# Two transformer blocks on one core: gates as one plus tanh, and the second group of Fox keys and queries split piece by piece

## What is computed

```python
h = rmsnorm(x, norm_mix)
q_a, k_a, v_a, f_a, q_b, kv_b, g_b, gate_a, gate_b = jnp.split(h @ w_in, ...)
log_f = log_sigmoid(f_a + b_forget)
o_a = fox_attention(q_a, k_a, v_a, log_f)      # 8 heads of 64, causal, decay by log_f
y_a = from_heads(o_a) @ w_o_fox
g = sigmoid(g_b)                               # weights of three NSA branches
o_n = nsa_attention(...)                       # compressed, selected, windowed
y_b = from_heads(o_n) @ w_o_nsa
mixed = sigmoid(gate_a) * y_a + sigmoid(gate_b) * y_b
x = x + mixed @ w_out
h = rmsnorm(x, norm_mlp)
x = x + square(relu(h @ w_up)) @ w_down
```

## Time and profile before

| | us |
|---|---|
| median of 3 runs | 2934.06 |
| lowest and highest | 2933.1, 2936.9 |
| the profiled execution | 2932.05 |
| its span, first to last instruction | 2930.2 |
| TensorE busy | 2775.1 |
| VectorE busy | 1503.6 |
| ScalarE busy | 1216.8 |
| mean granted clock of TensorE | 0.977 |

### The profile page before, as it was taken

One profiled execution on the slowest core, in us unless ns is written; L12 is line 12 of the kernel. 1 busy time (PEld: TensorE's weight loads), 2 busy tenths in 40 slices (PEclk: granted clock), 3 DMA queues, 4 the chain that ended last, 5 costly groups with the idle time before them and its releaser, 6 DMA issues.

```text
span 2930.2 us, 34957 instructions
## 1 busy us (share of the span) xinstructions
PE 2775.1 (95%) x13625; PEld 2282.6 (78%) x13625; DVE 1503.6 (51%) x2695; ACT 1216.8 (42%) x2169; POOL 132.2 (5%) x221
## 2 busy tenths in 40 slices
PE   7999999998999999989889999999989899999997
PEld 6777888886778888767777888888767677888886
DVE  6755433457554334566755643342566655553343
ACT  4553222245532222455656443242455756342231
POOL 1000000000000000011121000000010111000000
PEclk9899999999999999989999999999999999999999
DMA  4102232221022323211311223333212211333332
GB/s 128 41 23 87 97 96 99 95 82 45 23 90 95 100 94 101 83 50 58 94 44 44 87 88 99 95 100 94 83 41 75 80 37 51 93 101 94 100 94 79
DMA packets 186359, 231.42 MB, mean 79 GB/s; under 512 B 11874, under 2 KB 140356, under 8 KB 186196
## 3 DMA queue, kind: packets, MB, share of 16 engines
q1 hardware_dynamic: 184500, 225.95, 24.7%
q0 software_dynamic: 976, 1.32, 0.3%
q10 hardware_dynamic: 720, 1.92, 0.2%
HBM read 227.05 MB, written 2.11 MB: 78 GB/s over the span
## 4 chain that ended last, share of the span: by engine, by line
PE 79%; DVE 11%; ACT 5%; issue 4%; DMA 0%; POOL 0%; DVEq 0%; ACTq 0%; SPq 0%
PE bank L643 23%; PE bank L645 23%; PE bank L644 23%; DVE Wl L2110 2%; PE bank L803 1%; PE bank L858 1%; ACT Wh L1412 1%; DVE STT L2389 1%; PE bank L879 1%; PE bank L740 1%; DVE KAl L2814 1%; PE bank L880 1%; PE bank L921 1%; PE bank L1103 1%; PE bank L788 1%
## 5 line engine op out<-in xcount | busy, mean ns | idle before, releaser
L2110 DVE TENSOR_TENSOR Wl<-RAW,Wh 128x1024 fp32r<-128x1024 f32 (+3 forms) x434 | 511.3, 1200 | 388.8 <-ACT Wh L1412 388.0
L1412 ACT ACTIVATE Wh<-RAW 128x1024 fp32r<-128x1024 f32 (+3 forms) x434 | 438.6, 1033 | 367.7 <-PE bank L645 367.2
L643 PE MATMUL bank<-Hh,Wh 128*128 128x512 f32 (+1 forms) x976 | 396.3, 406 | 9.1 <-DVE Wl L2110 7.5
L645 PE MATMUL bank<-Hh,Wl 128*128 128x512 f32 (+1 forms) x976 | 385.9, 395 | 0.0
L644 PE MATMUL bank<-Hl,Wh 128*128 128x512 f32 (+1 forms) x976 | 385.5, 395 | 0.0
L643 PE MATMUL bank<-Wh,A 128*128 128x512 f32 x864 | 337.2, 390 | 0.0
L645 PE MATMUL bank<-Wh,A 128*128 128x512 f32 x864 | 336.3, 389 | 0.0
L644 PE MATMUL bank<-Wl,A 128*128 128x512 f32 x864 | 336.2, 389 | 0.0
L643 PE MATMUL bank<-HA,Wh 128*128 128x512 f32 x704 | 276.7, 393 | 7.0 <-DVE HA L2159 7.0
L645 PE MATMUL bank<-HA,Wl 128*128 128x512 f32 x704 | 275.6, 391 | 0.0
L644 PE MATMUL bank<-HA,Wh 128*128 128x512 f32 x704 | 275.5, 391 | 0.0
(11 more groups left out here) (371 smaller groups left out, 4357.3 us busy)
## 6 DMA issues: line engine op xcount, KB each, us to landing
RAW<-in_w_up_dram SPq DMA_DIRECT2D x108, 512.0 KB, 3.6
RAW<-in_w_down_dram SPq DMA_DIRECT2D x108, 512.0 KB, 3.8
RAW<-in_w_in_dram SPq DMA_DIRECT2D x90, 512.0 KB, 3.5
RAW<-in_w_gate_dram SPq DMA_DIRECT2D x44, 512.0 KB, 3.5
RAW<-in_w_out_dram SPq DMA_DIRECT2D x28, 512.0 KB, 3.8
RAW<-in_cmp_w_dram SPq DMA_DIRECT2D x16, 512.0 KB, 3.9
RAW<-in_w_o_fox_dram SPq DMA_DIRECT2D x8, 512.0 KB, 3.4
RAW<-in_w_o_nsa_dram SPq DMA_DIRECT2D x8, 512.0 KB, 3.4
```

Of the source, the lines that this page charges most:

```text
L643: pe.matmul(o, sh, mh, start=first, stop=False)
L645: return pe.matmul(o, sl, mh, start=False, stop=last)
L1412: sc.activation(M.Wh[:, v % NHL, 0:n], M.RAW[:, v % NRAW, 0:n], ACT.Copy).then_inc(G.w_hi, 1)
L2110: ve.tensor_tensor(M.Wl[:, v % NRAW, 0:n], M.RAW[:, v % NRAW, 0:n], M.Wh[:, v % NHL, 0:n].bitcast(F32), ALU.subtract).then_inc(G.w_lo, 1)
```

## The change

Two edits. The first: the sigmoids of the two gates become `tanh(x / 2)` on ScalarE, VectorE's product with the bank becomes `(tanh + 1) * bank` in one instruction, and the missing factor of one half is put into the split of the sum (MXh with a scale, MXl with a factor). The sigmoid of the branch weights at the forget gate stays. The second: for heads 4 to 7 the evacuation of a Fox key or query keeps only the product into TQ. Its pieces become a side of their own (`split_k`, `split_q`), begun there, which idles for one tick and then does one piece on each engine per tick. In TensorE's program idle sides of the same length keep the ticks in step. For heads 0 to 3 the pieces stay in one run, but each KAl piece now waits for its own KAh piece, where before two waited for the second of a pair.

```diff
-    def lin_t_units(name, kt, xh, xl, before=None, count=1):
+    def lin_t_units(name, kt, xh, xl, before=None, count=1, after=None):
...
+                    if after:
+                        after()
...
+        splits = []
+        lin_t(f"fk{l} 1", KD, M.Hh, M.Hl, after=lambda: splits.append(begin(idle(5))))
+        lin_t(f"fq{l} 1", KD, M.Hh, M.Hl, after=lambda: splits.append(begin(idle(3))))
         kc = lin_t_units(f"kc{l}", KD, M.Hh, M.Hl)
         next(kc)
+        drain(*splits)
...
-        def fox_q(c):
+        splits = []
+
+        def split_q(c, j, name):
+            yield
+            sc.wait_ge(*K.drained(name))
+            for x in range(2):
+                sc.activation(M.QA[c][0:64, 2 * j + x, :], M.TQ[64 * x:64 * x + 64, j, :], ACT.Copy).then_inc(*hi.up())
+                yield
+
+        def split_k(c, j, name):
+            yield
+            sc.wait_ge(*K.drained(name))
+            for x in range(2):
+                for r in (0, 64):
+                    sc.activation(M.KAh[c][r:r + 64, 2 * j + x, :], M.TQ[64 * x:64 * x + 64, j, :], ACT.Copy).then_inc(*hi.up())
+                    yield
+
+        def fox_part(split, c):
+
             def evac(j, name):
-                sc.wait_ge(*K.drained(name))
-                for x in range(2):
-                    sc.activation(M.QA[c][0:64, 2 * j + x, :], M.TQ[64 * x:64 * x + 64, j, :], ACT.Copy).then_inc(*hi.up())
-            return evac
-
-        def fox_k(c):
-            def evac(j, name):
-                sc.wait_ge(*K.drained(name))
-                for x in range(2):
-                    for r in (0, 64):
-                        i = sc.activation(M.KAh[c][r:r + 64, 2 * j + x, :], M.TQ[64 * x:64 * x + 64, j, :], ACT.Copy)
-                    i.then_inc(*hi.up())
+                if c:
+                    splits.append(begin(split(c, j, name)))
+                else:
+                    for _ in split(c, j, name):
+                        pass
             return evac
...
-                sc.activation(m, m, ACT.Sigmoid).then_inc(G.sig, 1)
+                sc.activation(m, m, ACT.Tanh, scale=0.5).then_inc(G.sig, 1)
...
-                sc.activation(M.MXh[t + j], M.M0[:, t + j, :], ACT.Copy).then_inc(*hi.up())
+                sc.activation(M.MXh[t + j], M.M0[:, t + j, :], ACT.Copy, scale=0.5).then_inc(*hi.up())
...
-        lin_t(f"fk{l} 1", KD, fox_k(1))
-        lin_t(f"fq{l} 1", KD, fox_q(1))
+        lin_t(f"fk{l} 1", KD, fox_part(split_k, 1))
+        lin_t(f"fq{l} 1", KD, fox_part(split_q, 1))
         kc = lin_t_units(f"kc{l}", KD, kc_evac)
         next(kc)
+        drain(*splits)
...
-        def fox_q(c):
-            def evac(j, name):
-                ve.wait_ge(G.fox_lo, fox_lo.n - 1)
-                by_token(M.TQ[:, j, :], name, n, 0.125)
-                for x in range(2):
-                    q = M.QA[c][:, 2 * j + x, :]
-                    i = lower(q[64:128, :], M.TQ[64 * x:64 * x + 64, j, :], q[0:64, :])
-                i.then_inc(*fox_lo.up())
-            return evac
-
-        def fox_k(c):
+        splits = []
+
+        def split_q(c, j):
+            yield
+            for x in range(2):
+                q = M.QA[c][:, 2 * j + x, :]
+                i = lower(q[64:128, :], M.TQ[64 * x:64 * x + 64, j, :], q[0:64, :])
+                if x:
+                    i.then_inc(*fox_lo.up())
+                yield
+
+        def split_k(c, j):
+            yield
+            for x in range(2):
+                for r in (0, 64):
+                    i = lower(M.KAl[c][r:r + 64, 2 * j + x, :], M.TQ[64 * x:64 * x + 64, j, :], M.KAh[c][r:r + 64, 2 * j + x, :])
+                    if x and r:
+                        i.then_inc(*fox_lo.up())
+                    yield
+
+        def fox_part(split, c, gain=None):
             def evac(j, name):
                 if c:
+                    ve.wait_ge(G.fox_lo, fox_lo.n)
+                elif split is split_q:
                     ve.wait_ge(G.fox_lo, fox_lo.n - 1)
-                by_token(M.TQ[:, j, :], name, n)
-                for x in range(2):
-                    ve.wait_ge(*hi.due())
-                    for r in (0, 64):
-                        i = ve.tensor_tensor(M.KAl[c][r:r + 64, 2 * j + x, :], M.TQ[64 * x:64 * x + 64, j, :],
-                                             M.KAh[c][r:r + 64, 2 * j + x, :].bitcast(F32), ALU.subtract)
-                i.then_inc(*fox_lo.up())
+                by_token(M.TQ[:, j, :], name, n, gain)
+                if c:
+                    splits.append(begin(split(c, j)))
+                else:
+                    for _ in split(c, j):
+                        pass
             return evac
...
-                i = ve.tensor_tensor(m, m, M.bank[K.of(name)][:, :], ALU.mult)
+                i = ve.scalar_tensor_tensor(m, m, 1.0, M.bank[K.of(name)][:, :], ALU.add, ALU.mult)
...
-                    lower(M.MXl[t + j], m0, M.MXh[t + j]).then_inc(*a_lo.up())
+                    lower(M.MXl[t + j], m0, M.MXh[t + j], 0.5).then_inc(*a_lo.up())
```

More of the change, by code:

```diff
@@ L1340, in tensor_program @@
         done.add((f"fox{l}", 0))
-        lin_t(f"fk{l} 1", KD, M.Hh, M.Hl)
-        lin_t(f"fq{l} 1", KD, M.Hh, M.Hl)
+        splits = []
+        lin_t(f"fk{l} 1", KD, M.Hh, M.Hl, after=lambda: splits.append(begin(idle(5))))
+        lin_t(f"fq{l} 1", KD, M.Hh, M.Hl, after=lambda: splits.append(begin(idle(3))))
         kc = lin_t_units(f"kc{l}", KD, M.Hh, M.Hl)
         next(kc)
+        drain(*splits)
         done.add((f"fox{l}", 1))
@@ L2045, in scalar_program @@
         begin(forget_side())
-        lin_t(f"fk{l} 0", KD, fox_k(0))
-        lin_t(f"fq{l} 0", KD, fox_q(0))
+        lin_t(f"fk{l} 0", KD, fox_part(split_k, 0))
+        lin_t(f"fq{l} 0", KD, fox_part(split_q, 0))
         fox = begin(fox_side())
         done.add((f"fox{l}", 0))
-        lin_t(f"fk{l} 1", KD, fox_k(1))
-        lin_t(f"fq{l} 1", KD, fox_q(1))
+        lin_t(f"fk{l} 1", KD, fox_part(split_k, 1))
+        lin_t(f"fq{l} 1", KD, fox_part(split_q, 1))
         kc = lin_t_units(f"kc{l}", KD, kc_evac)
         next(kc)
+        drain(*splits)
         done.add((f"fox{l}", 1))
@@ L3066, in vector_program @@
         begin(forget_side())
-        lin_t(f"fk{l} 0", KD, fox_k(0))
-        lin_t(f"fq{l} 0", KD, fox_q(0))
+        lin_t(f"fk{l} 0", KD, fox_part(split_k, 0))
+        lin_t(f"fq{l} 0", KD, fox_part(split_q, 0, 0.125))
         fox = begin(fox_side())
         done.add((f"fox{l}", 0))
-        lin_t(f"fk{l} 1", KD, fox_k(1))
-        lin_t(f"fq{l} 1", KD, fox_q(1))
+        lin_t(f"fk{l} 1", KD, fox_part(split_k, 1))
+        lin_t(f"fq{l} 1", KD, fox_part(split_q, 1, 0.125))
         kc = lin_t_units(f"kc{l}", KD, kc_evac)
         next(kc)
+        drain(*splits)
         done.add((f"fox{l}", 1))
```

## The result

The changed kernel takes **2890.43 us** (median of 4 runs, 2888.99 to 2891.26), the kernel before 2933.58 beside it (4 runs, 2932.14 to 2936.90). The ratio is 0.9851, with a 95% interval of 0.9834 to 0.9868: 43.2 us less, where 36 were predicted. The profiled execution took 2891.26 us, its span is 2889.1, and the mean granted clock rose from 0.977 to 0.986.

A forecast was written before the change was run, and what follows sets the result against it. TensorE, busy 95% of the span, was taken as the bound, so only its pauses and lower-clock time pay. Fox 16 + gates 20 = 36 us off 2932.05 gave 2896, plus 2.0 for the median: 2898 us, range 2878 to 2917.

The forecast's parts named there:

- The first turn: Second Fox group's first score block: TensorE resumes at 1272.2 instead of 1278.61, 6.4 us earlier; first-group waits add 1.8.
- The new pauses of 2.1, 0.2, 1.0, 0.9 and 1.0 us: TensorE's waits expected in the second Fox group's steps, since each carries one or two pieces in series.
- the split's own 4.2 us: Second Fox group's keys: left by the sixth block of 6.4 us pause and 3.2 us half clock, after new pauses.
- the prediction's signs: Signs of being right, among them TensorE's idle time in the Fox stage down from 21 to about 14 us.
- The steps of 1.55, 2.7, 1.3 and 3.4 us: Gate stage, per layer: gains at the 3.41 us pause, the 1505 and 1509 pair, 1561, and half clock behind 1510.
- the half clock behind 1458 and 1561: Gate stage: counted as no gain, because pauses of 1.9 and 1.2 us stay; only in the upper end.
- The price of a load: ScalarE: each removed table load priced at 1.3 us; 43 x 1.283 = 55 us, nearly all beside TensorE's work.
- rival d: Gates: each switch frees more than a load's 1.3 us, remaining pauses go too; 48 us gain, 2886, chance 0.04.
- (a): Fox stage: split pieces serialise, the second group gains nothing; 24 us gain left, 2910 us, chance 0.13.
- (b): Gates don't pay, as ScalarE waits for VectorE where a load goes; 20 us gain left, 2914 us, chance 0.09.
- (c): Pauses go nearly whole in both stages and the clock stays up; 67 us gain, 2865 us, chance 0.05.
- (e): Fox stage, 1264 to 1306: pauses in every step keep the clock low throughout; 7 us slower, 2941, chance 0.03.

The follow-up runs named there:

- Fox alone: The change with its gates put back to the sigmoid, against the kernel before: 2915.35 us, ratio 0.9936; again 2913.96 us, ratio 0.9937.
- two a tick: The change with two key pieces per tick instead of one, queries as in the change: 2889.94 us, ratio 0.9853 to the kernel before.
- A shift of one tick: The change with both Fox groups and the kc copies split, its Fox side starting scores one tick later: 2893.73 us, ratio 0.9869 to the kernel before.

## Why the prediction came out as it did

**The bound and the mechanism were right.** TensorE stayed busy 95% of the span with the same instructions, and each pause that the text said would shrink did. The first turn moved as worked out: counted from the first KAh it came 8.1 us earlier, 1.8 of it gained up to the first scores (1264.47 before, 1264.62 after) and 6.3 behind them, where 1.8 and 6.4 were written. The 1.8 came from other parts than written: 1.3 of pause and the whole half clock behind it in layer 0, less 1.1 for the new wait of the scores for QA, which the prediction didn't have. The new pauses of 2.1, 0.2, 1.0, 0.9 and 1.0 us (5.2 in all) were 1.60, 1.74, 0.89 and 1.61 (5.8), with one turn fewer that waits, so the steps do go partly in series. With what went before, the Fox stage gave 7.5 us in layer 0 and 9.4 in layer 1 where 8.0 were written.

That the split's own 4.2 us came out (6.3 less 2.0) is luck. The first new pause is already inside the 6.4, so the text's numbers give 6.4 + 3.2 less 3.1 for the four later pauses, 6.5 us; 4.2 is about what is left when the first 2.1 are taken off once more. Measured, the later pauses are 4.2 us and not 3.1, and the lower clock in that stretch gave back some 2.2 (4.2 less 2.0) and not 3.2. So TensorE's idle time in the Fox stage fell from 21 to 17.3 us and not to about 14, as the prediction's signs had it.

**The gates: pauses right, clock too small.** 3.41 went to 1.97 (about 1.9 written), the pair to 0.69 (0.2 written), 2.45 to 1.65 (1.15 written). The steps of 1.55, 2.7, 1.3 and 3.4 us measured 1.9, 2.7, 1.4 and 3.2. The step that failed is the sentence on the half clock behind 1458 and 1561: nothing was counted there "as pauses of 1.9 and 1.2 us stay". They stay, and in this profile the clock behind both is 1.00 (1450 to 1456 and 1546 to 1552). The first place gave 1.6 us; the stretch from 1561 to 1713 gave 3.2 instead of 0.9. With these two terms at what they measured, 3.9 us more, the gates are 14.0 us in layer 0 and not 10; in layer 1 they are 12.3. So the 7 us between the forecast and the result are 6 at the gates (26.3 instead of 20) and 1 in the Fox stages (16.9 instead of 16).

Which place keeps its lower clock isn't fixed. The kernel before has a stretch of it behind each of the two pauses at 1437 and 1458 (mean clock 0.72 from 1437 to 1443 and from 1458 to 1464). In the profile after, one is left, behind the 1.97 us pause at 1431.67 (1430 to 1438: 0.79). In the profile of the change run again, one is left too, but behind the next pause, 1.98 us long (1447 to 1453: 0.72). Up to the mark at 1474.92 the two gain the same, 11.0 and 11.2 us.

**The price of a load** was right for ScalarE: 43 x 1.283 = 55.2 us of the 57.9 by which its busy time fell. The rule of the Trainium skill's page "ScalarE: Activation LUTs", section "What ACT_TABLE_LOAD costs" (2.66 us for a switch, rival d), would have freed 114 us of ScalarE. The load's own 1283 ns agree; the second part isn't seen. Busy time can't show a drain, but the idle times don't show one either: 0.5 us before all 26 loads at exp and 0.4 before all 24 at the gates in the earlier trace rows, and the exp behind the load at 1453.01 starts 0.02 us after its end.

**The rivals.** (a), pieces that serialise wholly: no, the first turn came 6.8 us nearer to the matmul behind the Wl pause than before (25.4 to 18.6 us), Fox alone gives 17.4 and 19.2 us, and two a tick changed nothing. (b), gates that don't pay: no, 20.3 to 22.7 us alone. (c), all pauses gone: no (its 67 us below the median would be 2867; 2865 is counted from the profiled execution). (d): the time lies near its 2886, but by the clock and not by its mechanism, since the 1.97 and 1.65 us pauses are still there. (e), a low clock across the split stretch: no, it is at 1.00 from 1265 to 1310 in spite of four pauses of 0.9 to 1.7 us. That the tanh edit alone pays less than in the change, because the Fox stage with its long pauses can give clock back, stood in no case.

## What to carry to other kernels

Where side work is in step with the main stream, look at what stands ahead of the first link of a chain that TensorE will want, here the maximum of the first block: moving 2.8 us of work from before it to behind it brought the first turn 6.3 us nearer, of which the next steps took 2.0 back, and splitting that work finer than needed was worth nothing. Price a pause that goes together with the lower clock behind it, also where a shorter pause stays, and put the part of the clock into the range, because it isn't fixed by one profile. A shift of one tick moves every meeting with the weights' plan, so try it as a kernel of its own and don't price it by the one wait that it is meant for; here most of its cost was clock and not waits.

## What the runs showed of the hardware that was not expected

The clock behind a pause of the same length is not always the same. Behind the 3.08 us OAy pause of the kernel before it is 1.00 in layer 0 and 0.72 in layer 1:

```profile
1324.00:1332.00 8.00, 4.92 (x34) 4.34 (x34) 4.89 (x12) 5.08 (x13) 1.89 (x3) 1.00 0.04 15
2184.00:2190.00 6.00, 4.26 (x20) 3.92 (x21) 2.65 (x6) 2.75 (x7) 1.40 (x2) 0.72 0.01 3
```

In the change the same pause of 3.07 us has 0.72 behind it in layer 0 (1320 to 1326, above) and 1.00 in layer 1, while the 2.48 us pause has 1.00 in layer 0 and 0.57 in layer 1:

```profile
2092.00:2096.00 4.00, 3.64 (x10) 2.90 (x11) 3.76 (x9) 0.00 (x0) 0.00 (x0) 0.57 0.19 66
2158.00:2164.00 6.00, 5.53 (x38) 4.87 (x38) 3.28 (x8) 2.54 (x7) 1.22 (x2) 1.00 0.01 3
```

So in one layer or the other a pause is followed by 1.2 GHz for 3 to 4 us and costs 1.5 to 1.7 us more, with the same instructions around it. Two executions of the same kernel differ in this too, as with the 1.97 and 1.98 us pauses above. Which of the pauses is followed by it stays open. Shown is only that its length alone doesn't decide, and that in the change, with fewer long pauses, the two stages run at 0.99 where the kernel before has 0.96.
